# Expert weights made slot by slot, and U and V rows asked for in turn, in the retrieval stage of a one-layer decoder kernel

## The chip, the cores and the metric

The kernel runs on one core of one Trainium2 chip. The metric is the device time of one execution in microseconds (us); less is better.

## The reference, cut to what matters

One layer of a decoder works on 512 prompt tokens (behind 16 meta tokens) and 8 sample tokens, 1024 wide, all in float32. After an RWKV-7 group, differential attention, an output projection and a layer norm, every token goes through the product-key retrieval of experts ("PEER"). The change touches only this part:

```python
def block(xt):                      # xt: a block of tokens x 1024, after the first layer norm
    q = (xt @ wq).reshape(blk, PK_HEADS, 2, PK_DQ // 2)          # 8 heads
    s = jnp.einsum('thcd,hckd->thck', q, subkeys)
    s1, i1 = lax.top_k(s[:, :, 0], PK_TOPK)                      # 16 of 128
    s2, i2 = lax.top_k(s[:, :, 1], PK_TOPK)
    ...
    top_s, sel = lax.top_k(cand_s, PK_TOPK)                      # 16 of 256
    idx = jnp.take_along_axis(cand_i, sel, axis=-1)
    gate = jax.nn.softmax(top_s, axis=-1)
    act = jax.nn.gelu(jnp.einsum('thed,td->the', U[idx], xt), approximate=False)
    return jnp.einsum('the,thed->td', gate * act, V[idx])
```

U and V are tables of 16384 rows of 1024 float32 (4 KB a row). Each token needs 8 x 16 = 128 rows of each. A second layer norm of the token plus this sum gives the output.

## The kernel before, in words

The last phase, `phase_peer`, handles four tiles of 128 prompt tokens, a token to a partition. A tile has 128 slots (8 heads, called `part`, x 16 experts). For a slot, GpSimd issues two indirect gathers, one of U and one of V, each of 128 rows (512 KB), whose row numbers lie in one column of `idx` in SBUF. The U row of a token is multiplied with the token's vector and summed (the dot, L1820, one instruction on VectorE that reads two SBUF operands and leaves its sum through a short read-out). ScalarE takes the gelu (L1704), VectorE multiplies with the gate (L1829), ScalarE makes a diagonal matrix 128x128 of the weights (L1710), and TensorE multiplies this diagonal with the V rows into an accumulator in PSUM (L1605, four matmul instructions a slot).

The order on each engine is written out by hand. `schedule` runs over tiles `t` and over 32 groups `g` of `G` = 4 slots; each engine calls its own `gather` for the group and then pieces of other work: a step of the attention of the next tile (`attend`), the projections and the first layer norm of the next tile (`prep`), the top-16 selection of a head two heads ahead (`head`, four pieces to a head, almost all on VectorE), and the second layer norm of the tile before (`finish`). GpSimd has only the gathers, in the order of its function `group`: four U, then four V. The buffers are rings: `Ur` of `R` = 8 slots, `Vr` of `RV` = 7, diagonals of `DG` = 8. `s_dot` counts groups of dots, `s_gel` and `s_w` groups of weights, `s_free` slots whose matmuls are done. Before the first U of a group GpSimd waits for the dots of the group two before; before each V for the matmuls of the slot seven before. Semaphores `s_u[r]` and `s_vv[r]` tell the landing of each row buffer. At the end two more groups of four slots, with the row numbers in `idr`, serve the 8 sample tokens (8 tokens x 8 heads x 16 experts are laid on 64 partitions first and spread to 128 partitions x 8 slots); their weights go through `wsel` (L1881, L1882) and the matmuls of L1620. Then come the last two layer norms.

Of the kernel before, what the change touches and what calls it, by code (L numbers as in the profile page):

```python
# [11 lines left out]
ACT = mybir.ActivationFunctionType  # L12
# [3 lines left out]
P = 128  # L16
# [3 lines left out]
NT = SEQ // P  # L20
# [10 lines left out]
PKH, NKEY, TOPK = 8, 128, 16  # L31
NEXP = NKEY * NKEY
SLOTS = PKH * TOPK
# [1235 lines left out]
def phase_peer(nc, io, m):  # L1269
# [4 lines left out]
    with ctx:  # L1274
        sb = lambda n, s, dt=F32: ctx.enter_context(nc.sbuf_tensor("p_" + n, s, dt))
        sem = lambda n: ctx.enter_context(nc.semaphore("p_" + n))
        ps, c = m.ps, m.c
        G = 4
        R = 8
        RV = 7  # L1280
        PARTS = PKH
        GPP = TOPK // G
# [8 lines left out]
        junk = sb("junk", [P, D])  # L1291
        x1 = sb("x1", [P, 2, D])
# [27 lines left out]
        gate = sb("gate", [P, 2, SLOTS])  # L1320
        Ur = sb("Ur", [P, R, D])
        Vr = sb("Vr", [P, RV, D])
        dot = sb("dot", [P, R])
        gel = sb("gel", [P, R])
        wgt = sb("wgt", [P, R])
        DG = 8
        dg = sb("dg", [P, DG, P])
        idr = sb("idr", [P, PKH], I32)
# [27 lines left out]
        s_gate = sem("gate")  # L1356
        s_u = [sem(f"u{i}") for i in range(R)]
        s_vv = [sem(f"v{i}") for i in range(RV)]
        s_dot = sem("dot")
        s_gel, s_w, s_dg = sem("gel"), sem("w"), sem("dg")  # L1360
# [48 lines left out]
        @block.sync  # L1409
        def _(sp):  # L1410
            sp.dma_start(x1[:, 0, :], io["x_tok"][0:P, :]).then_inc(s_x, 16)
            for j, n in enumerate(("ln1_w", "ln1_b", "ln2_w", "ln2_b")):
                sp.dma_start(ln[LNROW * j:LNROW * j + 1, :], io[n].unsqueeze(0)).then_inc(s_ln, 16)
            sp.dma_start(skT[:, :, :], io["skT"]).then_inc(s_ld, 16)
            for t in range(1, NTT):
                n = rows_of(t)
                sp.wait_ge(s_sp, t)
                if t >= 2:
                    sp.wait_ge(s_y, t - 1)
                    sp.dma_start(io["y_out"][(t - 2) * P:(t - 1) * P, :], x1[:, t % 2, :]).then_inc(s_yo, 16)  # L1420
                    sp.wait_ge(s_yo, 16 * (t - 1))
                sp.dma_start(x1[0:n, t % 2, :], io["x_tok"][t * P:t * P + n, :]).then_inc(s_x, 16)

            own = lambda a: a[0:NB * PKH, NT % 2, 0:TOPK].rearrange("r (a w) -> r a w", a=2)
            sp.wait_ge(s_idx, PKH * NT + 1)
            sp.dma_start(idr[:, :], own(idx)).then_inc(s_rs, 16)
            sp.wait_ge(s_rs, 16)
            sp.wait_ge(s_gate, PKH * NT + 1)
            sp.dma_start(gtr[:, :], own(gate)).then_inc(s_rs, 16)
            for t in range(NTT - 2, NTT):  # L1430
                sp.wait_ge(s_y, t + 1)
                n = rows_of(t)
                sp.dma_start(io["y_out"][t * P:t * P + n, :], x1[0:n, t % 2, :]).then_inc(s_yo, 16)
            sp.wait_ge(s_yo, 16 * NTT)

        @block.gpsimd
        def _(pool):
            def row(table, dst, at, s_to):
                pool.indirect_dma_start(out=dst, out_offset=None, in_=io[table],  # L1439
                                        in_offset=bass.IndirectOffsetOnAxis(ap=at, axis=0)).then_inc(s_to, 16)  # L1440

            def group(g, index):
                for j in range(G * g, G * g + G):
                    if j == G * g and j >= R:
                        pool.wait_ge(s_dot, g - R // G + 1)
                    row("peer_u", Ur[:, j % R, :], index(j), s_u[j % R])
                for j in range(G * g, G * g + G):
                    if j >= RV:
                        pool.wait_ge(s_free, j - RV + 1)
                    row("peer_v", Vr[:, j % RV, :], index(j), s_vv[j % RV])  # L1450

            for t in range(NT):
                for part in range(PARTS):
                    pool.wait_ge(s_idx, PKH * t + part + 1)
                    for grp in range(GPP):
                        group((PARTS * t + part) * GPP + grp, lambda j: idx[:, t % 2, j - SLOTS * t:j - SLOTS * t + 1])
            pool.wait_ge(s_rs, 16)
            for half in range(2):
                group(PARTS * NT * GPP + half, lambda j: idr[:, j - SLOTS * NT:j - SLOTS * NT + 1])
# [165 lines left out]
        def _(act):  # L1625
# [72 lines left out]
                    act.activation(s[:, 4 * a:4 * a + 4, :], ps[:, a, :].rearrange("p (k t) -> p k t", k=4), ACT.Copy).then_inc(s_scc, 1)  # L1698

            def gather(t, part, grp):  # L1700
                g = (PARTS * t + part) * GPP + grp
                hs = slice(G * g % R, G * g % R + G)
                act.wait_ge(s_dot, g + 1)
                act.activation(gel[:, hs], dot[:, hs], ACT.Gelu).then_inc(s_gel, 1)  # L1704
                act.wait_ge(s_w, g + 1)
                for k in range(G):
                    j = G * g + k
                    if j >= DG:
                        act.wait_ge(s_free, j - DG + 1)
                    act.activation(dg[:, j % DG, :], c("ident"), ACT.Copy, scale=wgt[:, j % R:j % R + 1]).then_inc(s_dg, 1)  # L1710

            schedule(gather, finish, attend, head, prep)
            for half in range(2):
                g = PARTS * NT * GPP + half
                hs = slice(G * g % R, G * g % R + G)
                act.wait_ge(s_dot, g + 1)
                act.activation(gel[:, hs], dot[:, hs], ACT.Gelu).then_inc(s_gel, 1)
            root(1, NT, P)
            root(1, NTT, NB)
# [2 lines left out]
        def _(dve):  # L1722
# [91 lines left out]
                    scale(0, t + 1, x, n, s_x1)  # L1814

            def dots(g, x):
                for j in range(G * g, G * g + G):
                    r = j % R
                    dve.wait_ge(s_u[r], 16 * (j // R + 1))
                    ins = dve.tensor_tensor_reduce(Ur[:, r, :], Ur[:, r, :], x, 1.0, 0.0, ALU.mult, ALU.add, dot[:, r:r + 1])  # L1820
                ins.then_inc(s_dot, 1)
                dve.wait_ge(s_gel, g + 1)

            def gather(t, part, grp):
                g = (PARTS * t + part) * GPP + grp
                hs = slice(G * g % R, G * g % R + G)
                at = TOPK * part + G * grp
                dots(g, x1[:, t % 2, :])
                dve.tensor_tensor(wgt[:, hs], gel[:, hs], gate[:, t % 2, at:at + G], ALU.mult).then_inc(s_w, 1)  # L1829

            def finish(t, step):
                n = rows_of(t)
# [13 lines left out]
            def attend(t, g):  # L1846
# [20 lines left out]
                if g == 17:  # L1867
                    dve.wait_ge(s_heads_act, n_root(t))
                    link(dve.reciprocal(ost[:, 2, :], ost[:, 1, :]))
                    link(dve.tensor_tensor(heads(o), heads(o), ost[:, 2, :].unsqueeze(2).broadcast_to([P, NH, DV]), ALU.mult), s_heads_dve)  # L1870

            schedule(gather, finish, attend, head, prep)

            dve.wait_ge(s_repc, 1)
            for half in range(2):
                g = PARTS * NT * GPP + half
                hs = slice(G * g % R, G * g % R + G)
                dots(g, junk[:, :])
                if half == 0:
                    dve.wait_ge(s_rs, 32)  # L1880
                link(dve.tensor_tensor(wgt[:, hs], gel[:, hs], gtr[:, hs], ALU.mult))  # L1881
                link(dve.tensor_tensor(wsel[:, hs, :], wgt[:, hs].unsqueeze(2).broadcast_to([P, G, NB]),  # L1882
                                       c("gather").unsqueeze(1).broadcast_to([P, G, NB]), ALU.mult), s_ws)
# [9 lines left out]
def build(nc, io, upto=9, debug=None):  # L1893
    root = ExitStack()
    with root:
# [30 lines left out]
        with mid:  # L1926
# [21 lines left out]
            if upto <= 2:  # L1948
                return
        phase_peer(nc, io, m)  # L1950


# [63 lines left out]
```

## Time and profile before

| what | value |
|---|---|
| median of 3 runs | 2142.63 us (2140.63 to 2150.62) |
| the profiled execution | 2140.99 us, its span 2139.0 us |
| busy: TensorE matmul | 1808.6 us (85%) |
| busy: VectorE | 1464.2 us (68%) |
| busy: GpSimd | 1351.1 us (63%) |
| busy: ScalarE | 463.1 us (22%) |
| moved by DMA | 620.99 MB, 581.00 MB of it on GpSimd's queue |

How to read it: the profile is of one execution. The span is the time from the first to the last instruction; what lies around it is the difference to the execution's time. Busy is the time in which an engine ran an instruction; of matmuls it is only modelled. In the names, PE is TensorE, PEld its weight loads, DVE VectorE, ACT ScalarE, POOL GpSimd, SP SyncE. An instruction's idle time is that of its engine just before it, and the arrow names what ended it; "issue" means that nothing in the profile did. Instructions of the dots are called CUSTOM_DVE_ANT_0.

### The profile page before, as it was taken

The numbers are of one execution on the slowest core, as the hardware profiler recorded it, in microseconds if no ns is written. First come the engines' busy times: TensorE is split into PE (matmuls) and PEld (weight loads), VectorE is DVE, ScalarE is ACT, GpSimd is POOL, SyncE is SP. The second block draws the span as 40 slices with busy tenths as digits, with TensorE's granted clock in tenths as the row PEclk, the third lists the DMA queues.
The fourth block names the chain that finished last, engine by engine and source line by source line (L and its number), as shares of the span: only waits on it lengthen the run. The fifth ranks groups of instructions, "written<-read, shape, count | busy, mean of one in ns | idle before, by whom it ended". The sixth has DMA issues, their size and how long they took to land.

```text
span 2139.0 us, 21362 instructions
## 1 busy us (share of the span) xinstructions
PE 1808.6 (85%) x7178; PEld 979.6 (46%) x7178; DVE 1464.2 (68%) x3289; ACT 463.1 (22%) x1116; POOL 1351.1 (63%) x1289
## 2 busy tenths in 40 slices
PE   7978769898796578899788899878999977899787
PEld 5843338677673433345333344433443533335332
DVE  2668635546546667786878787677877587686766
ACT  0122310000001123322223332222332222121220
POOL 3887423223210377777777777777777777777775
PEclk9989969898997699999989999999999998899988
DMA  7453121121115499999999999999999999999997
GB/s 253 161 187 114 40 75 55 42 64 45 45 50 209 147 376 408 407 405 375 391 398 409 392 409 380 404 380 399 380 380 385 388 391 383 409 399 358 409 408 302
DMA packets 178204, 620.99 MB, mean 290 GB/s; under 512 B 20420, under 2 KB 23876, under 8 KB 177712
## 3 DMA queue, kind: packets, MB, share of 16 engines
q0 software_dynamic: 160672, 581.00, 71.0%
q1 hardware_dynamic: 17424, 38.63, 4.9%
q8 instruction: 58, 0.95, 0.2%
q14 instruction: 50, 0.41, 0.1%
HBM read 613.89 MB, written 5.59 MB: 290 GB/s over the span
## 4 chain that ended last, share of the span: by engine, by line
PE 21%; POOL 16%; DVE 12%; DMA 11%; issue 6%; ACT 2%; SPq 0%; DVEq 0%; POOLq 0%
PE ps L1605 15%; DMA p_Ur<-in_peer_u_dram,p_idx 11%; POOL p_Ur L1439 8%; POOL p_Vr L1439 8%; DVE p_Ur L1820 6%; PE ps L1533 2%; PE ps L1559 1%; ACT p_dg L1710 1%; PE ps L1503 1%; ACT p_gel L1704 1%; PE ps L1505 0%; DVE p_wgt L1829 0%; DVE p_x L1745 0%; DVE p_x L1730 0%; PE ps L1520 0%
## 5 line engine op out<-in xcount | busy, mean ns | idle before, releaser
L1605 PE MATMUL ps<-p_Vr,p_dg 128*128 128x512 f32 x2048 | 989.1, 640 | 195.8 <-ACT p_dg L1710 195.5
L1820 DVE CUSTOM_DVE_ANT_0 p_Ur<-p_Ur,p_x 128x1024 f32<-128x1024 f32 x512 | 617.1, 1225 | 257.9 <-DMA p_Ur<-in_peer_u_dram,p_idx 247.4
L1605 PEld LDWEIGHTS ps<-p_Vr,p_dg 128*128 128x128 f32 x2048 | 408.4, 204 | 741.1 <-issue 493.0
L1439 POOL DMA_INDIRECT p_Ur<-in_peer_u_dram,p_idx x512 | 521.3, 1018 | 256.4 <-issue 155.8
L1439 POOL DMA_INDIRECT p_Vr<-in_peer_v_dram,p_idx x512 | 540.2, 1055 | 157.8 <-issue 121.7
L1704 ACT ACTIVATE p_gel<-p_dot 128x4 f32<-128x4 f32 x128 | 26.3, 205 | 945.3 <-DVE p_dot L1820 945.3
L1710 ACT ACTIVATE p_dg<-table_long,p_wgt 128x128 f32<-128x128 f32 x512 | 163.6, 390 | 29.4 <-DVE p_wgt L1829 29.2
L1024 POOL DMA_INDIRECT vring<-in_cache_v_dram,idx x64 | 60.8, 950 | 148.0 <-PE ps L885 146.3
L275 PE MATMUL ps<-xT,w_ring 128*128 128x268 f32 x448 | 104.7, 397 | 10.5 <-DMA xT<-in_xT_dram 6.3
L300 PE MATMUL ps<-w_ring,xT 128*128 128x512 f32 (+1 forms) x224 | 105.5, 627 | 4.3 <-ACT kv L402 4.3
L275 PEld LDWEIGHTS ps<-xT,w_ring 128*128 128x128 f32 x448 | 87.0, 195 | 28.3 <-issue 6.3
L426 POOL DMA_INDIRECT kv<-in_cache_k_dram,idx x56 | 62.9, 1123 | 39.2 <-DVE idx L474 23.4
L1559 PEld LDWEIGHTS ps<-p_pr,wq 128*128 128x128 f32 x640 | 76.4, 197 | 8.9 <-issue 7.7
L1038 POOL TENSOR_TENSOR XT<-msk,table_short 128x512 f32<-128x512 f32 (+1 forms) x10 | 11.2, 1121 | 109.1 <-DVE msk L1073 109.1
L1559 PE MATMUL ps<-p_pr,wq 128*128 128x128 f32 (+1 forms) x640 | 76.5, 276 | 0.7 <-ACT p_pr L1677 0.7
L448 POOL TENSOR_TENSOR kv<-kv,w_out 128x512 f32<-128x512 f32 x56 | 72.0, 1288 | 4.0 <-DMA w_out<-q_rows 2.2
L885 PE MATMUL ps<-vring,w_out 128*8 128x128 f32 x512 | 67.6, 276 | 3.4 <-DVE U L1100 3.4
L300 PEld LDWEIGHTS ps<-w_ring,xT 128*128 128x128 f32 (+1 forms) x224 | 41.6, 191 | 59.9 <-issue 59.8
L1704 ACT ACT_TABLE_LOAD x51 | 65.4, 1283 | 0.9
L752 PE MATMUL ps<-XT,T 128*128 128x128 f32 (+1 forms) x368 | 60.2, 264 | 0.0
L1095 DVE TENSOR_TENSOR X<-ps,X 128x512 f32<-128x512 f32 (+1 forms) x36 | 23.0, 638 | 51.9 <-PE ps L752 51.8
L750 PE MATMUL ps<-T,XT 128*128 128x128 f32 (+1 forms) x288 | 53.1, 271 | 0.0
(364 smaller groups left out, 2080.8 us busy)
## 6 DMA issues: line engine op xcount, KB each, us to landing
w_ring<-in_w_in_dram SPq DMA_DIRECT2D x5, 2048.0 KB, 9.0
p_Ur<-in_peer_u_dram,p_idx POOLq DMA_INDIRECT x512, 6.6
p_Vr<-in_peer_v_dram,p_idx POOLq DMA_INDIRECT x512, 6.7
w_out<-in_w_out_dram SPq DMA_DIRECT2D x2, 2048.0 KB, 10.6
wq<-in_pk_wq_dram SPq DMA_DIRECT2D x1, 4096.0 KB, 22.8
xT<-in_xT_dram SPq DMA_DIRECT2D x4, 536.0 KB, 6.2
kv<-in_w_in_dram SPq DMA_DIRECT2D x1, 2048.0 KB, 12.5
w_out<-q_rows POOLq DMA_DIRECT2D x8, 256.0 KB, 3.6
```

Of the source, the lines that this page charges most:

```text
L275: mm = pe.matmul(ps[:, 2 * a + ct % 2, 0:HALF], w, xT[:, k, a * HALF:(a + 1) * HALF], start=(k == 0), stop=(k == KT - 1))
L300: mm = pe.matmul(ps[0:rows, 4 + n % 2, :], xT[:, k, tt * P:tt * P + rows], wr[:, g % 2, k, :], start=(k == 0), stop=(k == KT - 1))
L426: pool.indirect_dma_start(out=key_pages(p, 1)[:, 0, :], out_offset=None, in_=io["cache_k"], in_offset=bass.IndirectOffsetOnAxis(ap=m.idx[: ...
L448: pool.tensor_tensor(page, page, qb[:, b % 2, :], ALU.mult).then_inc(s_km, 1)
L885: mm = pe.matmul(ps[0:NB, 1, h * DV:(h + 1) * DV], zatt[:, g, h, NB - 1 - b:2 * NB - 1 - b], vring[:, p % VR, h * DV:(h + 1) * DV], start= ...
L1024: pool.indirect_dma_start(out=vring[:, p % VR, :], out_offset=None, in_=io["cache_v"], in_offset=bass.IndirectOffsetOnAxis(ap=m.idx[:, p:p ...
L1439: pool.indirect_dma_start(out=dst, out_offset=None, in_=io[table], in_offset=bass.IndirectOffsetOnAxis(ap=at, axis=0)).then_inc(s_to, 16)
L1559: mm = pe.matmul(ps[:, a, (f % 4) * P:(f % 4) * P + n], wq[:, k, f * P:(f + 1) * P], x1T[:, k, 0:n], start=(k == 0), stop=(k == KT - 1))
L1605: mm = pe.matmul(acc[:, a, :], dg[:, j % DG, :], Vr[:, j % RV, a * 512:(a + 1) * 512], start=(at == 0), stop=(at == SLOTS - 1), skip_group ...
L1704: act.activation(gel[:, hs], dot[:, hs], ACT.Gelu).then_inc(s_gel, 1)
L1710: act.activation(dg[:, j % DG, :], c("ident"), ACT.Copy, scale=wgt[:, j % R:j % R + 1]).then_inc(s_dg, 1)
L1820: ins = dve.tensor_tensor_reduce(Ur[:, r, :], Ur[:, r, :], x, 1.0, 0.0, ALU.mult, ALU.add, dot[:, r:r + 1])
```

## The change

GpSimd asks for U and V in turn, slot by slot, and waits for the single dot of the slot eight before. VectorE counts each dot on `s_dot`; it no longer waits for the gelu nor multiplies with the gate, but waits before a group for the gelus of the slots sixteen before, whose columns in `dot` it overwrites. ScalarE does for each slot the gelu, the gate product (a copy with the gate as scale) and the diagonal, with a wait for its own result between them. The small buffers `dot`, `gel` and `wgt` grow from 8 to `RC` = 16 columns. For the samples the weights stay in groups of four.

```diff
+        RC = 4 * G
+        dot = sb("dot", [P, RC])
...
             def group(g, index):
                 for j in range(G * g, G * g + G):
-                    if j == G * g and j >= R:
-                        pool.wait_ge(s_dot, g - R // G + 1)
+                    if j >= R:
+                        pool.wait_ge(s_dot, j - R + 1)
                     row("peer_u", Ur[:, j % R, :], index(j), s_u[j % R])
-                for j in range(G * g, G * g + G):
                     if j >= RV:
                         pool.wait_ge(s_free, j - RV + 1)
                     row("peer_v", Vr[:, j % RV, :], index(j), s_vv[j % RV])
...
             def gather(t, part, grp):                                    # ScalarE
-                g = (PARTS * t + part) * GPP + grp
-                hs = slice(G * g % R, G * g % R + G)
-                act.wait_ge(s_dot, g + 1)
-                act.activation(gel[:, hs], dot[:, hs], ACT.Gelu).then_inc(s_gel, 1)
-                act.wait_ge(s_w, g + 1)
+                if grp == 0:
+                    act.wait_ge(s_gate, PKH * t + part + 1)
                 for k in range(G):
-                    j = G * g + k
+                    at = TOPK * part + G * grp + k
+                    j = SLOTS * t + at
+                    col = slice(j % RC, j % RC + 1)
+                    act.wait_ge(s_dot, j + 1)
+                    act.activation(gel[:, col], dot[:, col], ACT.Gelu).then_inc(s_gel, 1)
+                    act.wait_ge(s_gel, j + 1)
+                    act.activation(wgt[:, col], gel[:, col], ACT.Copy, scale=gate[:, t % 2, at:at + 1]).then_inc(s_w, 1)
+                    act.wait_ge(s_w, j + 1)
                     if j >= DG:
                         act.wait_ge(s_free, j - DG + 1)
-                    act.activation(dg[:, j % DG, :], c("ident"), ACT.Copy, scale=wgt[:, j % R:j % R + 1]).then_inc(s_dg, 1)
+                    act.activation(dg[:, j % DG, :], c("ident"), ACT.Copy, scale=wgt[:, col]).then_inc(s_dg, 1)
...
             def dots(g, x):
+                if G * g >= RC:
+                    dve.wait_ge(s_gel, G * g - RC + G)
                 for j in range(G * g, G * g + G):
                     r = j % R
                     dve.wait_ge(s_u[r], 16 * (j // R + 1))
-                    ins = dve.tensor_tensor_reduce(Ur[:, r, :], Ur[:, r, :], x, 1.0, 0.0, ALU.mult, ALU.add, dot[:, r:r + 1])
-                ins.then_inc(s_dot, 1)
-                dve.wait_ge(s_gel, g + 1)
+                    dve.tensor_tensor_reduce(Ur[:, r, :], Ur[:, r, :], x, 1.0, 0.0, ALU.mult, ALU.add,
+                                             dot[:, j % RC:j % RC + 1]).then_inc(s_dot, 1)
 
             def gather(t, part, grp):                                    # VectorE
...
-                dots(g, x1[:, t % 2, :])
-                dve.tensor_tensor(wgt[:, hs], gel[:, hs], gate[:, t % 2, at:at + G], ALU.mult).then_inc(s_w, 1)
+                dots((PARTS * t + part) * GPP + grp, x1[:, t % 2, :])
```

## Rows read from the trace of the kernel before

**Rows 1.** The page, costliest groups: busy us, mean ns, idle before.

```profile
L1439 POOL DMA_INDIRECT p_Ur<-in_peer_u_dram,p_idx x512 | 521.3, 1018 | 256.4 <-issue 155.8
L1439 POOL DMA_INDIRECT p_Vr<-in_peer_v_dram,p_idx x512 | 540.2, 1055 | 157.8 <-issue 121.7
...
L1704 ACT ACT_TABLE_LOAD x51 | 65.4, 1283 | 0.9
```

**Rows 2.** Busy time by stretch: its length, each engine (instructions), granted clock, DMA.

```profile
core 0: us, PE busy (x) PEld busy (x) DVE busy (x) ACT busy (x) POOL busy (x), PEclk, DMA share, GB/s
850.00:900.00 50.00, 40.89 (x96) 17.68 (x96) 40.52 (x103) 16.18 (x41) 38.27 (x39) 0.93 1.03 408
...
1900.00:1950.00 50.00, 47.83 (x153) 24.30 (x152) 39.33 (x102) 11.98 (x31) 39.49 (x35) 0.90 0.96 362
...
724.00:2121.00 1397.00, 1201.96 (x3216) 549.07 (x3216) 1047.50 (x2632) 371.70 (x924) 1077.61 (x1040) 0.93 1.01 392
```

**Rows 3.** Who waited for whom, 780 to 2139 us: total us, times, longest.

```profile
ACT p_gel L1704 <- DVE p_dot L1820: 914.1, 123, 10.7
...
DVE p_Ur L1820 <- DMA p_Ur<-in_peer_u_dram,p_idx: 238.0, 126, 5.8
...
POOL p_Ur L1439 <- issue: 152.5, 500, 0.3
...
DVE p_wgt L1829 <- ACT p_gel L1704: 35.7, 124, 2.3
POOL p_Vr L1439 <- PE ps L1605: 35.7, 112, 1.5
```

**Rows 4.** The tile p_Ur: its issues, and their landing.

```profile
L1439 POOL DMA_INDIRECT p_Ur<-in_peer_u_dram,p_idx x512: 933/937/1990, 724.1 to 2093.1; - x171
...
DMA to landing us min/median/max: 4.5/6.6/9.4
```

**Rows 5.** Instructions in order of time, one group: start us, us, what.

```profile
870.00 0.94 POOL L1439 DMA_INDIRECT p_Vr<-in_peer_v_dram,p_idx  x1 [0.31 <-PE ps L1605]
870.42 1.23 DVE L1820 CUSTOM_DVE_ANT_0 p_Ur<-p_Ur,p_x 128x1024 f32<-128x1024 f32 x1 [2.77 <-DMA p_Ur<-in_peer_u_dram,p_idx]
871.24 1.22 POOL L1439 DMA_INDIRECT p_Vr<-in_peer_v_dram,p_idx  x1 [0.30 <-issue]
...
871.61 1.23 DVE L1820 CUSTOM_DVE_ANT_0 p_Ur<-p_Ur,p_x 128x1024 f32<-128x1024 f32 x1
...
872.77 0.94 POOL L1439 DMA_INDIRECT p_Vr<-in_peer_v_dram,p_idx  x1 [0.30 <-issue]
...
875.43 0.20 ACT L1704 ACTIVATE p_gel<-p_dot 128x4 f32<-128x4 f32 x1 [8.11 <-DVE p_dot L1820]
875.67 0.16 DVE L1829 TENSOR_TENSOR p_wgt<-p_gel,p_gate 128x4 f32<-128x4 f32 x1 [0.27 <-ACT p_gel L1704]
...
875.87 1.28 ACT L1710 ACTIVATE p_dg<-table_long,p_wgt 128x128 f32<-128x128 f32 x4 [0.23 <-DVE p_wgt L1829]
```

**Rows 6.** The same view of 951 to 961 us.

```profile
951.43 1.02 POOL L1439 DMA_INDIRECT p_Vr<-in_peer_v_dram,p_idx  x1 [0.30 <-issue]
...
951.68 1.22 DVE L1734 CUSTOM_DVE_ANT_0 p_junk<-p_x 128x1024 f32<-128x1024 f32 x1
...
952.75 0.96 POOL L1439 DMA_INDIRECT p_Vr<-in_peer_v_dram,p_idx  x1 [0.30 <-issue]
...
956.60 1.22 DVE L1820 CUSTOM_DVE_ANT_0 p_Ur<-p_Ur,p_x 128x1024 f32<-128x1024 f32 x1
...
957.75 1.22 DVE L1820 CUSTOM_DVE_ANT_0 p_Ur<-p_Ur,p_x 128x1024 f32<-128x1024 f32 x1
957.79 1.99 POOL L1439 DMA_INDIRECT p_Ur<-in_peer_u_dram,p_idx  x1 [0.30 <-issue]
```

**Rows 7.** The dots' line alone in the stage.

```profile
724.00:2121.00 1397.00, 628.74 (x1039) 0.93 1.01 392
```

**Rows 8.** The end: GpSimd's last U issue, and TensorE's last sample matmuls.

```profile
2114.08 0.93 POOL L1439 DMA_INDIRECT p_Ur<-in_peer_u_dram,p_idr  x1 [0.30 <-issue]
```

```profile
2122.64 7.03 PE L1620 MATMUL ps<-p_Vr,p_wsel 128*8 128x512 f32 x16 [1.63 <-DVE p_wsel L1882]
```

More of the change, by code:

```diff
@@ L1322, in phase_peer @@
         Vr = sb("Vr", [P, RV, D])
-        dot = sb("dot", [P, R])
-        gel = sb("gel", [P, R])
-        wgt = sb("wgt", [P, R])
+        RC = 4 * G
+        dot = sb("dot", [P, RC])
+        gel = sb("gel", [P, RC])
+        wgt = sb("wgt", [P, RC])
         DG = 8
@@ L1700, in gather @@
             def gather(t, part, grp):
-                g = (PARTS * t + part) * GPP + grp
-                hs = slice(G * g % R, G * g % R + G)
-                act.wait_ge(s_dot, g + 1)
-                act.activation(gel[:, hs], dot[:, hs], ACT.Gelu).then_inc(s_gel, 1)
-                act.wait_ge(s_w, g + 1)
-                for k in range(G):
-                    j = G * g + k
+                if grp == 0:
+                    act.wait_ge(s_gate, PKH * t + part + 1)
+                for k in range(G):
+                    at = TOPK * part + G * grp + k
[6 more added lines that the diff above has]
+                    act.wait_ge(s_w, j + 1)
                     if j >= DG:
                         act.wait_ge(s_free, j - DG + 1)
-                    act.activation(dg[:, j % DG, :], c("ident"), ACT.Copy, scale=wgt[:, j % R:j % R + 1]).then_inc(s_dg, 1)
+                    act.activation(dg[:, j % DG, :], c("ident"), ACT.Copy, scale=wgt[:, col]).then_inc(s_dg, 1)
             schedule(gather, finish, attend, head, prep)
             for half in range(2):
-                g = PARTS * NT * GPP + half
-                hs = slice(G * g % R, G * g % R + G)
-                act.wait_ge(s_dot, g + 1)
+                hs = slice(G * half, G * half + G)
+                act.wait_ge(s_dot, SLOTS * NT + G * half + G)
                 act.activation(gel[:, hs], dot[:, hs], ACT.Gelu).then_inc(s_gel, 1)
@@ L1819, in dots @@
                     dve.wait_ge(s_u[r], 16 * (j // R + 1))
-                    ins = dve.tensor_tensor_reduce(Ur[:, r, :], Ur[:, r, :], x, 1.0, 0.0, ALU.mult, ALU.add, dot[:, r:r + 1])
-                ins.then_inc(s_dot, 1)
-                dve.wait_ge(s_gel, g + 1)
+                    dve.tensor_tensor_reduce(Ur[:, r, :], Ur[:, r, :], x, 1.0, 0.0, ALU.mult, ALU.add,
+                                             dot[:, j % RC:j % RC + 1]).then_inc(s_dot, 1)
             def gather(t, part, grp):
-                g = (PARTS * t + part) * GPP + grp
-                hs = slice(G * g % R, G * g % R + G)
-                at = TOPK * part + G * grp
-                dots(g, x1[:, t % 2, :])
-                dve.tensor_tensor(wgt[:, hs], gel[:, hs], gate[:, t % 2, at:at + G], ALU.mult).then_inc(s_w, 1)
+                dots((PARTS * t + part) * GPP + grp, x1[:, t % 2, :])
             def finish(t, step):
@@ L1875, in _ @@
             for half in range(2):
-                g = PARTS * NT * GPP + half
-                hs = slice(G * g % R, G * g % R + G)
-                dots(g, junk[:, :])
+                hs = slice(G * half, G * half + G)
+                dots(PARTS * NT * GPP + half, junk[:, :])
+                dve.wait_ge(s_gel, SLOTS * NT + half + 1)
                 if half == 0:
```

## The prediction, made before the changed kernel was run

> **What bounds the kernel now.** I read the page first, then the stretches of the gather, then the waits, then single instructions.
>
> The page names the gather's two issues and VectorE's dots among its costliest lines, all in one stage. From 724 us to 2121 us GpSimd issues 1040 indirect gathers of 512 KB, a U and a V for each slot [rows 2]; only some 20 us follow. DMA's share reads 1.0 there, so the DMA engines look like the bound, but the share doesn't move with the work: it is 1.03 where 408 GB/s flow and 0.96 where only 362 do [rows 2]. What moves with the rate is the number of issues in 50 us, 39 against 35, and GpSimd's busy time for one, 0.98 against 1.13 us.
>
> The waits say the same. GpSimd spends 35.7 us before V issues that PE is named to have released, in 112 pieces: 0.32 us each. Where nothing released it, a piece is 0.30 us (152.5 us in 500) [rows 3]. So the slot is nearly always free when its turn comes, and 0.30 us is what each instruction costs to reach. The stage is then GpSimd's queue: 1040 x (0.30 + 1.036) = 1390 us of 1397, with 1077.61 us / 1040 = 1.036 from [rows 2]. VectorE idles 238 us for U rows and ScalarE 914 us for dots [rows 3]: neither sets the pace.
>
> An issue takes 0.933 to 1.99 us, median 0.937 [rows 4]. The 1024 of the main loop take 521.3 + 540.2 = 1061.5 us [rows 1]; at 0.935 they would take 957.4. So 104 us are excess, 0.81 us per group of four slots. Its source shows beside the dots [rows 5, 6]. Dot 1 of a group runs 870.42 to 871.65; the issue that starts at 871.24 lasts 1.22 instead of 0.94 and ends 0.81 after the dot. In another group dots follow at once, 0.03 us or less behind each other and 1.15 apart (956.60, 957.75); the issue of 957.79 starts 0.04 after a dot and lasts 1.99, again ending 0.81 after that dot's 958.97. So an issue needs something some 0.12 us after its start (0.935 - 0.81) that a running dot withholds to its end. An issue whose need falls before a dot's start, or after its end, isn't touched (870.00, 872.77). The squares of the layer norm, the same operation alone (951.68 to 952.90), fit: the issue at 951.43 wants it at 951.55, before; the one at 952.75 at 952.87 and loses 0.03.
>
> The Trainium skill has the rule (SBUF — State Buffer, Who interferes with whom): a VectorE instruction with two SBUF inputs contends with a GpSimd instruction that reads SBUF, and the one that issues second blocks fully. The trace agrees, with the 0.81 us after the dot's end. The rule speaks against any edit that puts more dots across issues, and gives no other sum than these rows.
>
> **The change, part by part.**
>
> *Earlier release of slots.* U slots free singly; weights come sooner. Both shorten waits that cost GpSimd about nothing: 35.7 - 112 x 0.305 = 1.5 us at most [rows 3]. I take 0. What hides it is the depth of the slots, 8 x 2.66 = 21 us; without it each late dot would hold GpSimd.
>
> *VectorE.* It loses the wait for gelu (35.7 us in 124 [rows 3]) and the gate product (0.16 us [rows 5]), 0.45 us per group, off the path while it idles for U. A count on each dot: no row shows a price; it lies between 0 and the 0.04 us that lie between an instruction and the next that depends on it (875.63 to 875.67 [rows 5]), x 384 = 15 us spread over the stage, hidden by VectorE's idle; I take 0, since those 0.04 us hold a whole hand-over. A new wait for the gelu of 16 slots back is long met.
>
> *ScalarE.* Per slot 0.205 gelu + some 0.2 for the product (a 128x1 instruction, like the gelu) + 0.39 diagonal, with three hand-overs of 0.04: 0.92 us, per group 3.7 against the 1.72 from 875.43 to 877.15 [rows 5]. Slots come every 2.66 us (two issues of 1.33): covered. Behind the waiting gelu stand its copies and exps, as now. The last diagonal of a group is ready 1.72 - 0.92 = 0.8 us sooner, the first by the three dots that it no longer waits for. TensorE, with 1.76 us a slot [rows 8], isn't the pace. Table loads: there are 51 for 128 gelus [rows 1] although four copies stand between any two, so copies call for none: unchanged.
>
> *New waits.* V of slot j waits for the product of j-7, and now every later U stands behind it. From V(j-7) to V(j) are 7 x 2.66 = 18.6 us; the chain from U's issue is 6.6 to land [rows 4] + 1.23 + 0.92 + 1.76 = 10.5. 8 us are left for a late VectorE or TensorE, more if the pace slows: 0, upper bound 5 us in each of 4 tile changes (20 us).
>
> *The tail.* The last U goes 3 places later in GpSimd's queue; it was issued at 2114.08, and the last 16 matmuls, which need its dot, began at 2122.64 [rows 8]. 3 x 1.28 = +3.8 us.
>
> *The order of issue.* This is the term that decides. Now the four U land together, at issue pace, so the four dots run as one train spaced 1.28, and the trains fall into step with the issues: in the group at 871 only the first dot costs (0.28), the others 0 [rows 5]. A late VectorE gives the train of 1.15 spacing that loses 1.05 more [rows 6]. After the change U land every second issue, every 2.5 us or more. VectorE has 1047.5 - 628.7 = 419 us of other work [rows 2, 7], 3.2 us a group, 3.1 after the change. Four dots and this are 8.0 of 10.3 us, so it must idle for landings inside the group: dots stand apart.
>
> A dot apart covers 1.22 of the 1.24 us between two needs. If its phase is anything, it costs 1.22 x 1.22 / (2 x 1.24) = 0.60 us; a dot right behind it costs 0; a third right behind costs 1.05, as in [rows 6]. One group by hand: needs every 1.24 from 0, U(k) lands 2.48k + 6.53 (6.65 less the 0.12), VectorE free at 8.47. Dot 0 8.47-9.69 pushes the need at 8.68 to 9.69 (1.01). Dot 1 ends at 10.91, before the need at 10.93. Dot 2 11.49-12.71 pushes 12.17 to 12.71 (0.54). Dot 3 13.97-15.19: needs at 13.95 and 15.19, free. Sum 1.55; carried on with 2.2 and 2.4 us of other work, the next two groups sum to 2.6 and 3.3. A locked pattern exists: each landing-paced dot costing x with x = 0.28 - 2x, 0.09. But the same equation one issue on, x = 1.525 - 2x, gives 0.51.
>
> Bounds: two pairs of dots, 2 x 0.60 = 1.2 us a group; four apart, 2.4. I take 1.8, since the 3.1 us of other work makes the first two dots a pair and leaves two apart: 3 x 0.60. 128 x 1.8 = 230, less 104: **+126 us**. With 128 x 1.2: +50; with 2.4: +203.
>
> Sum against the profiled execution (2140.99, span 2139.0; the median of runs is 1.6 us above): 2141 + 126 + 4 = 2271, and I say **2270**.
>
> **Rivals.**
>
> *Locked, faster (chance 0.09).* If dots settle at the 0.09 us phase: 512 x 0.09 = 46 us instead of 104, 2141 - 58 + 4 = 2087. It decides if VectorE comes to each dot before the row: other work + 1.22 under 2.57 us, so under 1.35 us a group. It is 3.1, so the first dot of nearly every group breaks the step. Any gain of earlier slots would end here too.
>
> *Nothing moves (0.06).* Either the collisions are as many (0.8 a group), or the DMA engines bind after all: 2141 + 4 = 2145. Against it: share 1.0 at 362 and 408 GB/s [rows 2]. The Trainium skill (DMA: Bandwidth & Descriptors, Where 436 GB/s comes from) puts HBM's share of a core at about 358 GB/s; then nothing would move and the time would be 2141, by its figure an estimate. The 392 GB/s of the stage [rows 2] exceed it, so the measurement decides.
>
> *Mild (0.08).* 0.9 to 1.15 a group: +11 to +43, some 2170.
>
> *My case (0.70).* 1.15 to 2.5 a group: 2190 to 2360.
>
> *More than that (0.07).* All four dots apart, and the V waits of tile changes on top: 2141 + 203 + 4 + 20 = 2368.
>
> **How the numbers follow.** 0.5%, 11 us, is what a measurement of this kernel can tell. Faster 0.09, same 0.06, slower 0.85. The range leaves out the faster and unmoved cases, part of the mild and the largest: 2165 to 2350, from 0.96 to 2.4 a group.
>
> **What would show it.** Right: issues still 1040, still 0.30 us apart without real waits; their mean up from 1.037 to about 1.16 us (+0.12); busiest stretches at 32 to 36 issues in 50 us, 340 to 375 GB/s; dots still 1.225 us, mostly preceded by an idle for U. Wrong: mean issue near 1.0 (locked); GpSimd waiting for matmuls or dots in pieces over 1 us (slots); ScalarE named before GpSimd. The size is the weak step: phases need not be random.

## The result, and the profile after

The changed kernel took 2221.14 us (median of 4 runs, 2214.99 to 2230.0) against 2146.62 us before on the same occasions: ratio 1.0346, 95% interval 1.0292 to 1.0400. It is slower by 3.5%, or some 75 us. The profiled executions are 2217.36 and 2140.99 us, 76.4 us apart; their spans 2215.2 and 2139.0.

The page's costliest groups of the changed kernel, in the columns of [rows 1]:

```profile
L1825 DVE CUSTOM_DVE_ANT_0 p_Ur<-p_Ur,p_x 128x1024 f32<-128x1024 f32 x512 | 621.1, 1226 | 403.8 <-DMA p_Ur<-in_peer_u_dram,p_idx 398.8
...
L1440 POOL DMA_INDIRECT p_Ur<-in_peer_u_dram,p_idx x512 | 547.8, 1070 | 256.1 <-issue 155.8
L1440 POOL DMA_INDIRECT p_Vr<-in_peer_v_dram,p_idx x512 | 588.4, 1149 | 156.1 <-issue 143.9
L1708 ACT ACTIVATE p_gel<-p_dot 128x1 f32<-128x1 f32 x512 | 103.3, 202 | 713.1 <-DVE p_dot L1825 712.0
L1714 ACT ACTIVATE p_dg<-table_long,p_wgt 128x128 f32<-128x128 f32 x512 | 205.6, 402 | 16.7
L1710 ACT ACTIVATE p_wgt<-p_gel,p_gate 128x1 f32<-128x1 f32 x512 | 150.8, 295 | 16.6
...
L1708 ACT ACT_TABLE_LOAD x51 | 65.4, 1283 | 49.2 <-DVE p_dot L1825 48.8
```

The 1024 issues take 547.8 + 588.4 = 1136.2 us; they took 1061.5 [rows 1]. That is 74.7 us more for the same 1024 instructions, and nearly all of the 76.4. The dot still takes 1.226 us.

Busy time by stretch, in the order of [rows 2]:

```profile
724.00:2196.00 1472.00, 1214.05 (x3211) 535.56 (x3212) 1027.63 (x2503) 637.80 (x1820) 1152.27 (x1040) 0.94 0.99 373
850.00:900.00 50.00, 37.49 (x88) 15.30 (x86) 35.25 (x91) 26.67 (x72) 39.12 (x36) 0.97 0.98 373
...
1900.00:1950.00 50.00, 41.45 (x92) 13.81 (x91) 34.08 (x88) 18.61 (x57) 39.39 (x35) 1.00 0.98 370
```

The stage holds the same 1040 issues in 75 us more. What was a quick stretch before (39 issues, 408 GB/s) has 36 and 373 GB/s; the slow one of before (35 issues) is as slow as it was. VectorE's busy time falls by 20 us, ScalarE's rises from 372 to 638 us.

Who waited for whom, 780 us to the end:

```profile
DVE p_Ur L1825 <- DMA p_Ur<-in_peer_u_dram,p_idx: 384.8, 290, 3.0
...
POOL p_Ur L1440 <- issue: 152.5, 500, 0.3
POOL p_Vr L1440 <- issue: 140.3, 460, 0.3
...
POOL p_Vr L1440 <- PE ps L1605: 12.2, 40, 0.3
```

GpSimd still waits for nothing: every piece is the 0.30 us that it takes to reach an instruction. VectorE's waits for U rows went from 126 pieces to 290 [rows 3], none longer than 3.0 us: the dots now come apart. What that does is seen in GpSimd's and VectorE's instructions in order of time:

```profile
876.92 1.23 DVE L1825 CUSTOM_DVE_ANT_0 p_Ur<-p_Ur,p_x 128x1024 f32<-128x1024 f32 x1
877.18 1.77 POOL L1440 DMA_INDIRECT p_Vr<-in_peer_v_dram,p_idx  x1 [0.31 <-PE ps L1605]
...
878.91 1.22 DVE L1825 CUSTOM_DVE_ANT_0 p_Ur<-p_Ur,p_x 128x1024 f32<-128x1024 f32 x1 [0.76 <-DMA p_Ur<-in_peer_u_dram,p_idx]
879.26 1.68 POOL L1440 DMA_INDIRECT p_Ur<-in_peer_u_dram,p_idx  x1 [0.30 <-issue]
...
881.25 0.94 POOL L1440 DMA_INDIRECT p_Vr<-in_peer_v_dram,p_idx  x1 [0.30 <-issue]
881.47 1.23 DVE L1825 CUSTOM_DVE_ANT_0 p_Ur<-p_Ur,p_x 128x1024 f32<-128x1024 f32 x1 [1.33 <-DMA p_Ur<-in_peer_u_dram,p_idx]
882.49 1.02 POOL L1440 DMA_INDIRECT p_Ur<-in_peer_u_dram,p_idx  x1 [0.30 <-issue]
```

The issue of 877.18 starts inside a dot that ends at 878.15 and ends 0.80 us after it; that of 879.26 ends 0.81 after the dot's 880.13. They have lost 0.83 and 0.75 us. The issue of 882.49 starts 0.21 before its dot's end and loses 0.08. It is the picture of [rows 5, 6], one dot at a time.

### The profile page after: what moved, and what is told of

Read it like the earlier page. It is cut to its first block, busy times and chain, and to the rows that moved or that the text cites. A ratio compares the mean times of both kernels' runs of the same rounds, so it can differ in the third digit from the quotient of the medians.

```text
span 2215.2 us, 22552 instructions
## 1 busy us (share of the span) xinstructions
PE 1824.1 (82%) x7178; PEld 967.5 (44%) x7178; DVE 1449.6 (65%) x3161; ACT 729.3 (33%) x2012; POOL 1426.7 (64%) x1289
## 4 chain that ended last, share of the span: by engine, by line
POOL 34%; PE 11%; issue 10%; DMA 7%; DVE 6%; ACT 1%; SPq 0%; DVEq 0%; POOLq 0%; ACTq 0%
POOL p_Vr L1440 18%; POOL p_Ur L1440 16%; PE ps L1605 8%; DMA p_Ur<-in_peer_u_dram,p_idx 6%; DVE p_Ur L1825 2%; PE ps L1559 1%; PE ps L1533 1%; ACT p_dg L1714 0%; PE ps L1503 0%; DVE p_x L1748 0%; PE ps L1620 0%; DMA p_Ur<-in_peer_u_dram,p_idr 0%; DVE p_x L1752 0%; ACT p_wgt L1710 0%; PE ps L1467 0%
## 5 line engine op out<-in xcount | busy, mean ns | idle before, releaser
L1605 PE MATMUL ps<-p_Vr,p_dg 128*128 128x512 f32 x2048 | 1004.7, 639 | 254.3 <-ACT p_dg L1714 252.4
L1605 PEld LDWEIGHTS ps<-p_Vr,p_dg 128*128 128x128 f32 x2048 | 395.6, 202 | 826.3 <-ACT p_dg L1714 420.1
L1440 POOL DMA_INDIRECT p_Ur<-in_peer_u_dram,p_idx x512 | 547.8, 1070 | 256.1 <-issue 155.8
L1440 POOL DMA_INDIRECT p_Vr<-in_peer_v_dram,p_idx x512 | 588.4, 1149 | 156.1 <-issue 143.9
L1708 ACT ACTIVATE p_gel<-p_dot 128x1 f32<-128x1 f32 x512 | 103.3, 202 | 713.1 <-DVE p_dot L1825 712.0
L1714 ACT ACTIVATE p_dg<-table_long,p_wgt 128x128 f32<-128x128 f32 x512 | 205.6, 402 | 16.7
L1710 ACT ACTIVATE p_wgt<-p_gel,p_gate 128x1 f32<-128x1 f32 x512 | 150.8, 295 | 16.6
L1708 ACT ACT_TABLE_LOAD x51 | 65.4, 1283 | 49.2 <-DVE p_dot L1825 48.8
```

What stands on the lines that cost most here:

```text
L1605: mm = pe.matmul(acc[:, a, :], dg[:, j % DG, :], Vr[:, j % RV, a * 512:(a + 1) * 512], start=(at == 0), stop=(at == SLOTS - 1), skip_group ...
L1708: act.activation(gel[:, col], dot[:, col], ACT.Gelu).then_inc(s_gel, 1)
L1710: act.activation(wgt[:, col], gel[:, col], ACT.Copy, scale=gate[:, t % 2, at:at + 1]).then_inc(s_w, 1)
```

## The experiments

Each time stands beside runs of the kernel before on the same chip (medians 2146.62 us for the changed kernel, 2145.46 for the four below it, 2151.08 for the next four, 2146.52 for the last two); the ratio is to those. The times are medians of four to twelve runs, of two for the one-operand and half-dot kernels. The mean issue is the mean duration of GpSimd's 1040 gathers in the one profiled execution.

| kernel | time, us | ratio (95%) | mean issue, us |
|---|---|---|---|
| changed | 2221.14 | 1.0346 (1.0292 to 1.0400) | 1.108 |
| order in turn alone | 2244.01 | 1.0461 (1.0422 to 1.0499) | 1.101 |
| weights by slot alone | 2139.15 | 0.9980 (0.9955 to 1.0004) | 1.027 |
| one operand, before | 2112.65 | 0.9855 (0.9821 to 0.9888) | 0.947 |
| one operand, changed | 2105.86 | 0.9823 (0.9785 to 0.9860) | 0.946 |
| train, in turn | 2255.1 | 1.0528 (1.0458 to 1.0597) | 1.033 |
| pairs | 2184.66 | 1.0173 (1.0101 to 1.0246) | 1.076 |
| gap, before | 2162.29 | 1.0068 (1.0038 to 1.0099) | 1.040 |
| gap, weights by slot | 2146.69 | 0.9989 (0.9957 to 1.0021) | 1.037 |
| filler, weights by slot | 2139.68 | 0.9952 (0.9928 to 0.9977) | 1.030 |
| half dots, changed | 2104.23 | 0.9789 (0.9731 to 0.9847) | 0.982 |

**The order alone.** The kernel before with the two loops of `group` made one:

```diff
                     row("peer_u", Ur[:, j % R, :], index(j), s_u[j % R])
-                for j in range(G * g, G * g + G):
                     if j >= RV:
```

> The kernel before with one thing changed: U and V are asked for in turn; dots, gelu, gate product and diagonal stay in groups of four, and the wait for dots stays one per group. Theory 1 (dots that stand apart hold up GpSimd's issues): the whole loss comes with it: the mean issue rises from 1.037 to about 1.11 us, the time from 2141 to about 2215 (2200 to 2235), like the changed kernel. Theory 2 (the longer chain on ScalarE and the single counts cost the time): no more than 5 us over before. Theory 3 (GpSimd waits for slots): pieces over 1 us in front of V issues named to matmuls.

The order alone costs more than the whole change, 4.6%, and 9 us more than the top of the expected range. Its page and its waits from 780 to 2139 us say how:

```profile
L1439 POOL DMA_INDIRECT p_Ur<-in_peer_u_dram,p_idx x512 | 547.1, 1069 | 257.8 <-issue 157.4
L1439 POOL DMA_INDIRECT p_Vr<-in_peer_v_dram,p_idx x512 | 581.4, 1136 | 187.8 <-issue 124.4
```

```profile
POOL p_Vr L1439 <- PE ps L1604: 60.0, 97, 4.6
```

The issues lengthen by 67 us over those of before (1128.5 less 1061.5; 74.7 in the changed kernel). On top come real waits for V slots: 60.0 - 97 x 0.305 = 30 us. So theory 1 holds for its part, and theory 3 has a part of its own that I had given to neither kernel: with the weights made only when the fourth dot of a group is done, a V slot is late for an order in turn. The trace says which: nearly all of this waiting (31 pieces) stands before the fourth V of a group, whose buffer is that of the first slot of the group before.

**The weights alone.** The changed kernel with the second loop of `group` put back:

```diff
                     row("peer_u", Ur[:, j % R, :], index(j), s_u[j % R])
+                for j in range(G * g, G * g + G):
                     if j >= RV:
```

> The changed kernel with one thing undone: four U, then four V, as before; counts per dot, weights slot by slot on ScalarE and single U slots stay. Theory 1: the loss is gone: mean issue 1.03 to 1.04 us, time 2135 to 2147. Theory 2: it stays at 2210 or more, ScalarE in the chain. A small gain under 0.5% is open, since VectorE has 0.45 us a group less to do.

2139.15 us, ratio 0.998, not told apart from before. ScalarE's longer chain and the single counts cost nothing that shows. With the first run this splits the change: the order costs some 99 us (2244 less 2145), the weights by slot give back 23 of them (2244 to 2221; the waits of 30 us are gone, the issues are 8 us longer), and without the order they are worth nothing that shows. "Weights by slot" here is the whole rest of the change, with the single U slots and the 16 columns; no run takes it apart.

**Dots with one SBUF operand.** In both kernels each dot became a sum over the U row alone; the product with the token's vector is left out:

```diff
-                    dve.tensor_tensor_reduce(Ur[:, r, :], Ur[:, r, :], x, 1.0, 0.0, ALU.mult, ALU.add,
-                                             dot[:, j % RC:j % RC + 1]).then_inc(s_dot, 1)
+                    dve.tensor_reduce(dot[:, j % RC:j % RC + 1], Ur[:, r, :], AX.X, ALU.add).then_inc(s_dot, 1)
```

> The kernel before, each dot replaced by a plain sum of the U row (one SBUF operand; the product with the token's vector is left out). Theory 1, with the skill's rule that only a second SBUF operand contends: no issue is held, mean 0.94 to 0.95 us, the stage falls from 1396 to 1040 x 1.245 = 1295 us, the time to about 2040 (2030 to 2055), unless the DMA engines bind at over 409 GB/s. Rival (any VectorE instruction holds the issue, or long issues come from full DMA rings): mean still above 1.02 us, time above 2120.

> The changed kernel with the same replacement of the dots by a plain sum of the U row (the product with the token's vector is left out). Theory 1: it falls to the same time as the one above, about 2040 (2030 to 2060), so by 175 us, and the order of issue makes no difference any more but for the 4 us of the tail. Rival: it stays 50 us or more above the one above.

The page of the second of them:

```profile
L1825 DVE TENSOR_REDUCE p_dot<-p_Ur 128x1 f32<-128x1024 f32 x520 | 621.3, 1217 | 309.8 <-DMA p_Ur<-in_peer_u_dram,p_idx 295.7
...
L1440 POOL DMA_INDIRECT p_Ur<-in_peer_u_dram,p_idx x512 | 484.3, 946 | 258.8 <-issue 135.8
L1440 POOL DMA_INDIRECT p_Vr<-in_peer_v_dram,p_idx x512 | 484.3, 946 | 201.0 <-issue 120.1
```

The sums take 1.217 us, nearly as long as the dots, and there are as many, yet the issues are at 0.947 in one kernel and 0.946 in the other: 968.6 us for 1024 where the changed kernel had 1136.2. So a busy VectorE alone does not hold an issue. The order makes no difference any more that shows, 2113 and 2106 us.

The edit takes away two things, though: the second SBUF operand, and the writing of 1024 products back to SBUF. Other instructions in the same trace part the two. The squares of the layer norm still read two SBUF operands, and still hold issues. The additions at the end of a layer norm write 512 columns each, read one operand from SBUF and one from PSUM, and hold none:

```profile
951.25 1.23 DVE L1737 CUSTOM_DVE_ANT_0 p_junk<-p_x 128x1024 f32<-128x1024 f32 x1
951.64 1.65 POOL L1440 DMA_INDIRECT p_Ur<-in_peer_u_dram,p_idx  x1 [0.30 <-issue]
...
1429.44 1.28 DVE L1752 TENSOR_TENSOR p_x<-p_x,ps 128x512 f32<-128x512 f32 x2
1429.62 0.94 POOL L1440 DMA_INDIRECT p_Vr<-in_peer_v_dram,p_idx  x1 [1.82 <-PE ps L1605]
```

Over all twelve traces, counting issues that start well inside such an instruction (0.04 us or more after its start, 0.18 or more before its end), the squares held 42 of 42, the dots 2604 of 2630, the one-operand sums none of 784, and the three kinds of instruction that read PSUM beside SBUF and write 512 columns none of 155. So it is the second SBUF operand and not the write. It isn't the only thing that holds an issue: an addition of one number per row to 1024 columns (TENSOR_SCALAR, one SBUF operand of that size, 0.75 us) held 26 of 28. There are eight of these in a kernel.

The Trainium skill's rule (SBUF — State Buffer, Who interferes with whom) says that an instruction with two SBUF inputs contends with a GpSimd instruction that reads SBUF and that one with a single SBUF input, outside its faster two-port modes, does not. Both runs agree with it. The same section infers that generating a DMA's descriptors needs the pair's write side, by which an instruction that only has two inputs would not hold up a DMA; for these gathers, whose row numbers lie in SBUF, it does.

My 2040 us was wrong, though. GpSimd's pace was not free to go to 1.245 us. A stretch of the second, and its waits:

```profile
1300.00:1350.00 50.00, 49.86 (x228) 30.69 (x227) 30.29 (x40) 24.34 (x73) 35.94 (x39) 1.00 1.03 408
```

```profile
POOL p_Vr L1440 <- PE ps L1605: 79.4, 120, 5.2
```

The rate stays at 408 GB/s, 1.28 us for 512 KB, and GpSimd now does wait for slots (43 us beyond the 120 x 0.305). So a second bound lies some 33 to 40 us under the kernel before. Its page also has the median time from issue to landing, 9.4 us for U and V alike, where it was 6.6 and 6.7 us before:

```profile
p_Ur<-in_peer_u_dram,p_idx POOLq DMA_INDIRECT x512, 9.4
```

A slow chain from a landing to a free slot would not lengthen the transfers. They pile up, so the second bound is in moving the rows; whether the DMA engines or the memory sets it, no run here separates.

**Half dots.** The changed kernel, each dot over 512 of the 1024 columns (the other half of the product is left out):

```diff
-                    dve.tensor_tensor_reduce(Ur[:, r, :], Ur[:, r, :], x, 1.0, 0.0, ALU.mult, ALU.add,
+                    dve.tensor_tensor_reduce(Ur[:, r, 0:512], Ur[:, r, 0:512], x[:, 0:512], 1.0, 0.0, ALU.mult, ALU.add,
```

> The changed kernel, order in turn kept, each dot over the first 512 of the 1024 columns only (the other half of the product is left out), so about 0.69 us long and not 1.23. Theory 1: a dot holds an issue less often and for less: 0.34 x (0.69 / 1.23)^2 = 0.11 us for one that stands apart, mean issue 0.96 to 0.99 us, and the pace then is set by the landing of rows at 409 GB/s as with one operand: 2095 to 2125. Rival (the order itself is dear): over 2180.

2104 us with a mean issue of 0.982, the order still in turn. The dots take 0.692 us and one that stands apart costs 0.07 us on average, against 0.34. Time and mean issue lie in the expected ranges. The order is dear only by what a dot covers.

**Pairs.** Two U, two V (the first of the inner loops asks for U, the second for V):

```diff
+                for p in range(G * g, G * g + G, 2):
+                    for j in (p, p + 1):
...
+                    for j in (p, p + 1):
```

> The changed kernel with the order two U, two V. U land in pairs, so about two separate hits a group instead of three, at 0.34 us each and fewer trains of three dots. Theory 1: mean issue 1.04 to 1.08 us, time between the order of four and the order of one: 2150 to 2200. Rival without a link to the dots: either of the ends, 2139 or 2217.

2184.66 us, mean issue 1.076: between the two orders (2139 and 2221) in both.

**A train in the order in turn.** The changed kernel; VectorE starts a group only with its fourth U landed, and each dot waits for the end of the one before:

```diff
+                last = G * g + G - 1
+                dve.wait_ge(s_u[last % R], 16 * (last // R + 1))
                 for j in range(G * g, G * g + G):
...
+                    if j > G * g:
+                        dve.wait_ge(s_dot, j)
```

> The changed kernel, U and V still in turn, but VectorE waits for the landing of the group's fourth U before its first dot, and each further dot waits for the end of the one before. So the dots no longer stand apart; they run as one train whose spacing rises from 1.15 to about 1.26 us, just over the 1.24 us of an issue. Theory 1 (what costs is a dot that stands apart, not the order as such): each group pays one hit of 0.3 to 0.6 us, the mean issue falls from 1.11 to 0.98 to 1.02 us and the time to 2090 to 2150. Rival (the order as such, U and V alternating on the DMA engines or in GpSimd's queue): time stays at 2200 or more. Second rival: VectorE's extra waiting makes slots late, GpSimd waits for matmuls in pieces over 1 us.

The first half came out in direction: the mean issue fell from 1.108 to 1.033 us, 78 us over 1040, with U and V still in turn, though not to the 0.98 to 1.02 expected. The time did not follow, 2255 us and not 2090 to 2150, since the second rival came too:

```profile
POOL p_Vr L1440 <- PE ps L1605: 124.9, 135, 5.5
```

By this row, which covers 780 to 2120 us, 124.9 - 135 x 0.305 = 84 us are real waits for V slots, again nearly all before the fourth V of a group. Holding the dots together buys the issues back and pays with late slots. So the issues' length hangs on the spacing of the dots and not on the order; the time of this kernel alone would not have shown it.

**A gap between dots, and a filler.** In [rows 6] a late train spaced 1.15 us costs most at its third dot. Three kernels try to widen the spacing, two by a gap (a dot waits for the end of the dot before; the kernel before counts these ends on a semaphore of their own) and one by a filler, 8 columns that nobody reads:

```diff
+                    if j > G * g:
+                        dve.wait_ge(s_dot, j)
...
+                    if j < G * g + G - 1:
+                        dve.memset(pad[:, j % RC, :], 0.0)
```

> The kernel before with one addition: within a group each dot waits for the end of the one before it, so that a train that starts late is spaced 1.26 us and not 1.15. Theory 1: the third dot of a late train no longer holds an issue for 0.9 us (31 such, 28 us in the trace of before); mean issue 1.037 to about 1.01, time 2110 to 2130. Rival (the spacing does not matter, or VectorE gets late from 0.3 us a group more): 2140 or more.

> The changed kernel with the order four U, four V, and within a group each dot waits for the end of the one before it. Theory 1: as the kernel above, with 0.45 us a group less on VectorE: 2105 to 2130, the best of all. Rival: no better than the order alone restored, 2135 or more.

> The changed kernel with the order four U, four V, and an independent short instruction of VectorE (a fill of 8 columns nobody reads) after each of the first three dots of a group. Waiting for a dot's end gave a spacing of 1.37 us, more than the 1.24 of an issue, and each dot of a train then held an issue for 0.13; a filler should give 1.20 to 1.30 us. Theory 1: if the spacing comes out at 1.24 to 1.29, late trains keep step with the issues, mean issue 1.00 to 1.02 us, time 2110 to 2130. If it comes out under 1.24 or over 1.32, no gain over the order alone restored (2139). Rival (spacing does not matter): 2139 at any spacing.

The gap missed in both kernels: 2162 and 2147 us. VectorE's instructions of the first of them:

```profile
874.68 1.23 DVE L1824 CUSTOM_DVE_ANT_0 p_Ur<-p_Ur,p_x 128x1024 f32<-128x1024 f32 x1 [2.37 <-DMA p_Ur<-in_peer_u_dram,p_idx]
875.83 0.08 DVE L1824 DVE_READ_ACCUMULATOR2_ANT p_dot<- 128x1 f32 x1
876.05 1.23 DVE L1824 CUSTOM_DVE_ANT_0 p_Ur<-p_Ur,p_x 128x1024 f32<-128x1024 f32 x1
```

A dot that waits for the one before starts 1.37 or 1.38 us after it, not 1.26. That is 0.14 over the 1.24 of an issue, and now every dot of a train holds its issue for that: 358 of the 1040 issues took 1.0 to 1.1 us (59 before), and these 0.4 us a group use up what was to be gained at the third dots (28 us over 128 groups, 0.22). The sum of the 1040 issues is 1081.2 us against 1077.6 before. That is only 4 of the 17.6 us by which this profiled span is longer; most of the rest, some 14 us, are real waits for V slots. With the weights by slot the gap adds 10 us of issues to the 1068.4 without it. The filler lands at the other side. VectorE's instructions with it:

```profile
880.65 1.23 DVE L1827 CUSTOM_DVE_ANT_0 p_Ur<-p_Ur,p_x 128x1024 f32<-128x1024 f32 x1 [2.06 <-DMA p_Ur<-in_peer_u_dram,p_idx]
...
881.82 1.21 DVE L1827 CUSTOM_DVE_ANT_0 p_Ur<-p_Ur,p_x 128x1024 f32<-128x1024 f32 x1
881.84 0.07 DVE L1830 MEMSET p_pad<- 128x8 f32 x1
...
883.07 1.23 DVE L1827 CUSTOM_DVE_ANT_0 p_Ur<-p_Ur,p_x 128x1024 f32<-128x1024 f32 x1
```

The fill runs beside the tail of a dot, so the spacing is 1.17 us in some pairs and 1.22 to 1.29 in others, in part under what was aimed at; it leaves the mean issue at 1.030, no shorter than the 1.027 without it. With 0.9952 (0.9928 to 0.9977) it is the only kernel with the whole work that is told apart from before on the faster side, by half a per cent; as its issues are no shorter than those of the weights alone, the filler is not shown to be the reason.

## Why the prediction was right, and what was off

- *GpSimd's queue is the bound; DMA and the other engines are not.* Right. With shorter issues the time fell in both orders. But the next bound is near: no stretch of 50 us in any kernel goes over about 410 GB/s, and with free issues the time stops 33 to 40 us below the kernel before.
- *A running dot withholds what an issue needs 0.12 us after its start.* Right that a dot holds issues, and right at the dot's end; wrong at its start. With one SBUF operand the issues fell to 0.946 us with VectorE's instructions about as long and as many; with half dots to 0.982. But an issue that starts up to 0.12 us before a dot, and so has its need inside it, should lose 1.1 us or more by this step, and it loses nothing. The changed kernel has 39 such issues and the kernel before 81, and they lose 0.01 us on average:

```profile
885.06 0.94 POOL L1440 DMA_INDIRECT p_Ur<-in_peer_u_dram,p_idx  x1 [0.30 <-issue]
885.13 1.23 DVE L1825 CUSTOM_DVE_ANT_0 p_Ur<-p_Ur,p_x 128x1024 f32<-128x1024 f32 x1 [2.42 <-DMA p_Ur<-in_peer_u_dram,p_idx]
```

  In five traces put together (before, changed, pairs, order alone, weights alone) none of the issues that start under 0.04 us after a dot's start is held, and all that start 0.05 or more after it are, until about 0.12 before the dot's end. So the one that starts second waits, as the rule that the prediction quotes has it, and a dot can hold an issue in 1.06 us of its 1.225, not in 1.22.
- *Dots would stand apart.* Right: 290 waits for U rows instead of 126. I put each issue's excess over 0.935 us to the dot that runs 0.12 us after its start. Before, 168 dots stood apart from the one ahead by 1.35 us or more, after the change 419 of 520, that is 3.2 a group; I had counted two and a pair, so 3.
- *0.60 us for each.* This step failed in size. It is the term of the sum for the order: I took the phase as random, and 3 x 0.60 = 1.8 us a group. The 419 dots cost 143 us, 0.34 each. The miss has two parts. The shorter stretch makes the random value 1.06 x 1.06 / (2 x 1.24) = 0.46 and not 0.60, an estimate by the formula of the prediction. And the phases are not random: 146 of the 419 start within 0.2 us of a need that has just been met, where some 60 would by chance (0.2 of the 1.41 us from issue to issue), and there they hold the next issue little; 160 of the 419 cost under 0.1 us. So the step of 0.09, which I had named as a state that other work would break, may come back between the breaks; that the dots settle there is not shown. Against this, dots right behind another (24 us) and VectorE's other instructions (13 us) stood at 0 in the sum. All in all the term came to (1136.2 - 957.4) / 128 = 1.40 us a group instead of 1.8, +74.7 us instead of +126, and the mean issue, said to reach 1.16 us, reached 1.108. The range held it; the point was 49 us too high.
- *The tail, +3.8.* From the last issue's start to the span's end it took 2139.0 - 2119.3 = 19.7 us before and 2215.2 - 2192.5 = 22.7 after: +3.0.
- *Slot waits, 0.* Right for the changed kernel (12.2 us in 40 pieces of 0.30), but without the weights by slot the order in turn waits 30 us, which the sum did not say.
- *ScalarE.* The gate product took 0.295 us and not 0.2; the chain from gelu to the end of the diagonal 0.96 us (880.18 to 881.14) against 0.92. Off the path, as the weights alone showed.
- *VectorE's relief and the count per dot, 0.* Right within 0.5%: 0.998 (0.9955 to 1.0004).

## What to carry to other kernels

When GpSimd issues the gathers, look at the duration of its issues beside VectorE's instructions with two SBUF operands before you change an order: the queue may be the bound though it waits for nothing and though DMA's share reads 1.0. A change that makes rows arrive evenly can spread such instructions over more issues; in this kernel trains that kept step with the issues were cheaper. Before you price a collision, look in the trace for the issues that start just before and just after such an instruction and read off which of them lose time: the width of the stretch that collides enters squared. And take the phases from the trace too; here a random phase came out too dear.

## What the runs had of the hardware that I had not expected

A VectorE instruction that waits for the end of a dot before it starts 1.37 or 1.38 us after that dot's start, 0.15 us after its end, where the same pair without the wait is 1.15 apart. A fill of 8 columns takes 0.065 us. The TENSOR_SCALAR over 1024 columns can hold an issue late as well: in the changed kernel six of them start 0.4 us after an issue's start, and each time that issue lasts 1.27 us and ends 0.12 after it. A dot that starts so late leaves the issue as it is: 50 issues with a dot 0.3 to 0.5 us after their start, and none over them before, lost 0.01 us on average. And ScalarE's table loads: this line has 51 in every kernel, but where ScalarE idled 0.9 us in all ahead of them [rows 1], it now idles 49.2 us, 48.8 of them until a dot. So part of the loads stand behind the wait for the dot, and their 1.283 us follow it instead of running ahead of it. It cost nothing here, since ScalarE had room.
